# Routed expert blocks in pairs: TensorE's order of products, transposes and down products

## The reference

```python
scores = sigmoid(u @ w_router)                # 512 tokens, 64 experts
top_e  = ...                                  # 8 experts for each token, from the best 4 of 8 groups
wts    = scores[top_e] / sum * 2.5
# for each expert e and the tokens that chose it:
hid = silu(x @ we_gate[e]) * (x @ we_up[e])   # 1024 -> 256
y  += (hid @ we_down[e]) * wts                # 256 -> 1024
h   = h + g2 * (y + shared expert)
out = rmsnorm(h, final_norm_g)
```

## Time and profile before

| what | value |
|---|---|
| median of 3 executions | 2199.33 us (2198.82 to 2207.7) |
| the profiled execution | 2204.64 us, span 2202.8 us |
| mean granted TensorE clock | 0.990 |
| TensorE busy | 2139.4 us, 97% |
| VectorE, ScalarE, GpSimd busy | 55%, 33%, 38% |
| DMA | 358.78 MB, mean 163 GB/s |

### The profile page before, as it was taken

One profiled execution on the slowest core, in us unless ns is written; L12 is line 12 of the kernel. 1 busy time (PEld: TensorE's weight loads), 2 busy tenths in 40 slices (PEclk: granted clock), 3 DMA queues, 4 the chain that ended last, 5 costly groups with the idle time before them and its releaser, 6 DMA issues.

```text
span 2202.8 us, 31560 instructions
## 1 busy us (share of the span) xinstructions
PE 2139.4 (97%) x11812; PEld 1526.5 (69%) x11813; DVE 1214.1 (55%) x1894; ACT 716.2 (33%) x1116; POOL 839.5 (38%) x600
## 2 busy tenths in 40 slices
PE   6999999999989999999999999999999999999998
PEld 5877667787868777777777778876555555555554
DVE  6567665789991448599999684246421212121213
ACT  4335663333341324344444345223111111111112
POOL 4331023434443324334334356532144444444443
PEclk9999899999999999999999999999999999999999
DMA  5230122454544322333333313321768899999885
GB/s 166 77 96 1 68 77 77 148 196 153 191 144 144 105 60 78 105 101 102 104 101 101 96 58 114 116 101 77 293 221 289 302 335 307 319 341 343 318 296 195
DMA packets 172306, 358.78 MB, mean 163 GB/s; under 512 B 18785, under 2 KB 108001, under 8 KB 153393
## 3 DMA queue, kind: packets, MB, share of 16 engines
q1 hardware_dynamic: 136880, 256.81, 33.1%
q0 software_dynamic: 28336, 85.91, 12.6%
q10 hardware_dynamic: 6992, 14.75, 1.9%
HBM read 390.15 MB, written 33.10 MB: 192 GB/s over the span
## 4 chain that ended last, share of the span: by engine, by line
PE 85%; DMA 5%; DVE 3%; ACT 2%; POOL 2%; issue 1%; SPq 1%; ACTq 0%; POOLq 0%; DVEq 0%
PE bank L933 25%; PE bank L1667 14%; PE bank L1356 12%; PE bank L1688 7%; PE bank L1255 4%; PE bank L1435 3%; DMA arena<-in_we_gate 2%; PE bank L1646 2%; PE bank L1069 1%; PE bank L1442 1%; DMA arena<-in_w_up 1%; PE bank L1520 1%; PE bank L942 1%; PE bank L1104 1%; PE bank L950 1%
## 5 line engine op out<-in xcount | busy, mean ns | idle before, releaser
L1667 PE MATMUL bank<-arena,hn 128*64 128x256 f32 x3072 | 346.1, 384 | 6.2 <-DMA arena<-in_we_gate 5.5
L1667 PEld LDWEIGHTS bank<-arena,hn 128*64 128x64 f32 x3072 | 225.5, 139 | 139.0 <-issue 35.4
L813 POOL TENSOR_TENSOR w_low_flat<-arena,in_high 128x1024 fp32r<-128x1024 f32 x71 | 184.3, 2617 | 278.5 <-ACT in_high L1996 278.4
L2951 DVE TENSOR_TENSOR inv<-inv,bank 128x128 f32<-128x128 f32 x96 | 23.2, 283 | 321.4 <-PE bank L1667 321.4
L1688 PE MATMUL bank<-arena 128*64 128x512 f32 x768 | 175.4, 598 | 0.3 <-DVE arena L2957 0.3
L780 POOL TENSOR_TENSOR w_low<-arena,w_high 128x2048 fp32r<-128x2048 f32 x22 | 103.6, 4709 | 160.2 <-ACT w_high L1918 160.2
L1356 PE MATMUL bank<-in_x,in_high 128*128 128x512 f32 x384 | 154.2, 402 | 0.0
L2965 DVE SCALAR_TENSOR_TENSOR sq<-bank,arena 128x512 f32<-128x512 f32 x96 | 72.1, 751 | 148.6 <-PE bank L1688 143.7
L1356 PE MATMUL bank<-in_x,w_low_flat 128*128 128x512 f32 x384 | 151.1, 393 | 0.0
L1356 PE MATMUL bank<-x_low,in_high 128*128 128x512 f32 x384 | 150.7, 392 | 0.0
L933 PE MATMUL bank<-x_high,w_high 128*128 128x512 f32 x336 | 133.4, 397 | 1.9 <-POOL w_low L780 1.9
(11 more groups left out here) (506 smaller groups left out, 4912.5 us busy)
## 6 DMA issues: line engine op xcount, KB each, us to landing
arena<-in_we_gate SPq DMA_DIRECT2D x49, 1024.0 KB
arena<-in_we_up SPq DMA_DIRECT2D x49, 1024.0 KB
arena<-in_w_in SPq DMA_DIRECT2D x38, 1024.0 KB, 5.4
arena<-in_w_ada SPq DMA_DIRECT2D x12, 2048.0 KB, 8.0
arena<-in_w_up SPq DMA_DIRECT2D x22, 1024.0 KB, 10.7
arena<-in_w_in SPq DMA_DIRECT2D x17, 512.0 KB, 5.3
arena<-in_w_out SPq DMA_DIRECT2D x4, 2048.0 KB, 9.9
arena<-in_w_down SPq DMA_DIRECT2D x4, 2048.0 KB, 9.6
```

Source lines behind the costliest of these rows:

```text
L813: pool_eng.tensor_tensor(in2_tile(j, "low"), in2_tile(j, "whole"), in2_tile(j, "high").bitcast(f32), ALU.subtract).then_inc(S("w_low"), 1)
L1667: ins = nc.tensor.matmul(rows_of(banks[2 + part][:, 0:FE], c), columns_of(moe["xT"][:, p, :], k, c), moe["gu"][:, 2 * p + c, at:at + FE], ...
```

## The change

TensorE's order becomes: gate and up products of the pair's two blocks; then all transposes (the next pair's first block, half 0; hidden of the first block; half 1; the next pair's second block, half 0; hidden of the second block; half 1); then the down products of both blocks. The second block's down sums go to banks 3 and 1. The waits are set anew for the shared banks, and ScalarE's and VectorE's orders follow the pair. The orders of GpSimd and of the sync engine's queue are not in the diff. Its core:

```diff
+        DOWN_BANKS = ((5, 6), (3, 1))
...
@@ TensorE: block_transposes(b, p, gathers, half) @@
                 if half == 0:
                     pe.wait_ge(S(f"x_gathered{p}"), gathers * 16)
+                if p == 1:
+                    pe.wait_ge(S("xT_done"), b * 2 + (half - 1))
+                elif half == 1:
+                    pe.wait_ge(S("y_copied"), b * 2 + (2 * TT - 4))
@@ TensorE: block_up(b, p) @@
                     pe.wait_ge(S(f"{name}_in"), needed)
+                    if p == 0 and part == 1:
+                        pe.wait_ge(S("y_copied"), b * 2 + (2 * TT - 1))
+                    if p == 1:
+                        pe.wait_ge(*((S("gate_through"), b + 2) if part == 0 else (S("moe_hid"), b * 2)))
@@ TensorE: down_free is gone; the rest @@
-            def down_free(b, loaded, value):
-                pe.wait_ge(S(loaded), value)
-                for half in range(2):
-                    pe.wait_ge(S("y_copied"), b * 2 + (2 * TT + half - 1))
-
             def hidden_transposes(b, p):
+                if p == 1:
+                    pe.wait_ge(S("hT_done"), b * 2)
...
-            def block_down(b, p):
+            def block_down(b, p, loaded, value, copied=None):
+                pe.wait_ge(S(loaded), value)
                 for k in range(2):
                     pe.wait_ge(S("hT_done"), b * 2 + (k + 1))
                     for half in range(2):
+                        if k == 0 and half == 1 and copied is not None:
+                            pe.wait_ge(S("xT_done"), copied)
...
-                            ins = nc.tensor.matmul(rows_of(banks[5 + half], c), columns_of(moe["hidT"][:, p, :], k, c),
+                            ins = nc.tensor.matmul(rows_of(banks[DOWN_BANKS[p][half]], c), columns_of(moe["hidT"][:, p, :], k, c),
...
-            def block(b, p, gathers, loaded, value):
-
-                block_up(b, p)
-                block_transposes(b + 1, 1 - p, gathers, 0)
-                hidden_transposes(b, p)
-                down_free(b, loaded, value)
-                block_transposes(b + 1, 1 - p, gathers, 1)
-                block_down(b, p)
-
-            for half in range(2):
-                block_transposes(0, 0, 1, half)
-            block(0, 0, 1, "we_down_in", 32)
-            block(1, 1, 2, "we_down_in", 64)
+            def pair_rest(b, gathers, loaded, values):
+
+                block_transposes(b + 2, 0, gathers, 0)
+                hidden_transposes(b, 0)
+                block_transposes(b + 2, 0, gathers, 1)
+                block_transposes(b + 3, 1, gathers, 0)
+                hidden_transposes(b + 1, 1)
+                block_transposes(b + 3, 1, gathers, 1)
+                block_down(b, 0, loaded[0], values[0])
+                block_down(b + 1, 1, loaded[1], values[1], b * 2 + 8)
+
+            for p in range(2):
+                for half in range(2):
+                    block_transposes(p, p, 1, half)
+                block_up(p, p)
+            pair_rest(0, 2, ("we_down_in", "we_down_in"), (32, 64))
             with pe.Fori(1, pairs_but_one) as i:
 
-
-                for p in range(2):
-                    block(i * 2 + p, p, i + (p + 1), f"down_loaded{p}", i * 32)
-            block(pairs_but_one * 2, 0, pairs, "down_loaded0", pairs_but_one * 32)
-            block_up(pairs_but_one * 2 + 1, 1)
-            hidden_transposes(pairs_but_one * 2 + 1, 1)
-            down_free(pairs_but_one * 2 + 1, "down_loaded1", pairs_but_one * 32)
-            block_down(pairs_but_one * 2 + 1, 1)
+                block_up(i * 2, 0)
+                block_up(i * 2 + 1, 1)
+                pair_rest(i * 2, i + 2, ("down_loaded0", "down_loaded1"), (i * 32, i * 32))
+            for p in range(2):
+                block_up(pairs_but_one * 2 + p, p)
+                hidden_transposes(pairs_but_one * 2 + p, p)
+                block_down(pairs_but_one * 2 + p, p, f"down_loaded{p}", pairs_but_one * 32)
@@ ScalarE: the loop @@
-            with act.Fori(1, pairs) as i:
-                for b, p in ((i * 2 + (-1), 1), (i * 2, 0)):
-                    block_gate(b, p)
-                    block_rows(b + 1, 1 - p)
+            with act.Fori(1, pairs_but_one) as i:
+                for p in range(2):
+                    block_gate(i * 2 + p, p)
+                for p in range(2):
+                    block_rows(i * 2 + (2 + p), p)
@@ VectorE: block_out reads DOWN_BANKS[p][half]; the loop @@
-            with dve.Fori(1, pairs) as i:
-                for b, p, added in ((i * 2 + (-1), 1, i), (i * 2, 0, i + 1)):
-                    block_hidden(b, p)
-                    block_hidden_T(b, p)
-                    block_out(b, p, added)
+            with dve.Fori(0, pairs_but_one) as i:
+                for p in range(2):
+                    block_hidden(i * 2 + p, p)
+                for p in range(2):
+                    block_hidden_T(i * 2 + p, p)
+                for p in range(2):
+                    block_out(i * 2 + p, p, i + 1)
```

More of the change, by code:

```diff
@@ L2288, in _ @@
             pairs = pairs_but_one + 1
-            block_rows(0, 0)
-            block_gate(0, 0)
-            block_rows(1, 1)
-            with act.Fori(1, pairs) as i:
-                for b, p in ((i * 2 + (-1), 1), (i * 2, 0)):
-                    block_gate(b, p)
-                    block_rows(b + 1, 1 - p)
-            block_gate(pairs_but_one * 2 + 1, 1)
+            for p in range(2):
+                block_rows(p, p)
+                block_gate(p, p)
+            for p in range(2):
+                block_rows(2 + p, p)
+            with act.Fori(1, pairs_but_one) as i:
[4 more added lines that the diff above has]
+            for p in range(2):
+                block_gate(pairs_but_one * 2 + p, p)
             nc.scalar.activation(RECIP[:, 0:TT], EPS_COLUMN.to_broadcast([P, TT]), ACT.Sqrt)
@@ L2964, in block_out @@
                     dve.wait_ge(S(("moe_y", "down_through")[half]), b + (1 + 2 * half))
-                    nc.vector.scalar_tensor_tensor(moe["y"][:, p, 512 * half:512 * half + 512], banks[5 + half][:, :],
+                    nc.vector.scalar_tensor_tensor(moe["y"][:, p, 512 * half:512 * half + 512], banks[DOWN_BANKS[p][half]][:, :],
                                                    moe["wcol"][:, p:p + 1], moe["g2"][:, 512 * half:512 * half + 512],
@@ L2975, in _ @@
             pairs = pairs_but_one + 1
-            block_hidden(0, 0)
-            block_hidden_T(0, 0)
-            block_out(0, 0, 1)
-            with dve.Fori(1, pairs) as i:
-                for b, p, added in ((i * 2 + (-1), 1, i), (i * 2, 0, i + 1)):
-                    block_hidden(b, p)
-                    block_hidden_T(b, p)
-                    block_out(b, p, added)
+            with dve.Fori(0, pairs_but_one) as i:
+                for p in range(2):
+                    block_hidden(i * 2 + p, p)
+                for p in range(2):
+                    block_hidden_T(i * 2 + p, p)
+                for p in range(2):
+                    block_out(i * 2 + p, p, i + 1)
+            block_hidden(pairs_but_one * 2, 0)
+            block_hidden_T(pairs_but_one * 2, 0)
+            block_out(pairs_but_one * 2, 0, pairs)
             dve.wait_ge(S("w_known"), pairs_but_one * 2 + 3)
```

## The result

The changed kernel takes 2421.63 us (median of 4 executions, 2418.41 to 2430.11); the kernel before took 2201.83 us on the same chip. The ratio is 1.1002, with a 95% interval of [1.098, 1.1024]. It is slower, as forecast, but by 220 us where 140 were forecast, and 2421.63 lies 10 us above the stated range.

What follows compares the result with a forecast made beforehand. TensorE's order was the bound, with GpSimd's unchanged order now stalling it: 22 x (5.1 + 1.7) = +150 us, gaps -7, gate-weight waits -9, end +6, together +140, so about 2339 us; range 2252 to 2412.

Steps and rivals of the forecast that it cites:

- D to first scatter: GpSimd, from the end of the first block's down products (D) to that block's scatter starting: 4.9 us.
- interval of the scatters: GpSimd, start of a pair's first scatter to start of its second: 9.4 us, about halfway between 7.3 and 11.75.
- second scatter to gather: GpSimd, from the second scatter's start to the issue of the pair's second gather: 2.8 us.
- landing of the gather: Second gather, from issue to rows landed: 7.0 us taken; the chain's gather took 6.21, the upper estimate was 9.
- wanted at: When TensorE needs the second gather: 19.0 us after the end of the first block's down products.
- clock: TensorE after each stall runs mostly at 1.2 GHz instead of 2.4: 1.7 us more per pair.
- TensorE's gaps: Gaps before hidden transposes and down products go in the new order: 0.3 us gained per pair, 7 us in all.
- GpSimd's instructions alone: Rival: GpSimd's instructions alone set the stall, scatters land quietly, clock stays up; 22 x 3.5 us, 2266 us; chance 0.15.
- The waits for gate weights: TensorE's two waits for gate weights (5.5 us) and their slow stretches go: -9 us.
- The end: Tail of the kernel: the scatter of block 46 waits for that of block 45, +6 us.
- The signs: Expected in the trace: about 22 gather waits of 3 to 9 us, 28 to 33 us per pair, DMA share about 0.75.
- the contention does not thin out: Rival: scatter intervals of 11.75 us and a gather landing of 9; 22 x (9.4 + 1.7), 2433 us; chance 0.13.

Runs made afterwards that it cites:

- The first experiment: Changed kernel with GpSimd's loop alone reordered, both gathers for the next pair issued ahead of the down load and scatter: 2213.9 us, ratio 1.0062.
- shorter warm products: Changed kernel with 8 unread products of 512 columns put before TensorE's wait for the second gather: 2391.39 us, ratio 1.0871.
- light weights: Changed kernel with its loop's gate and up loads cut to one eighth of their bytes, GpSimd's order unchanged: 2307.32 us, ratio 1.0483.
- hidden transposes apart, first run: Kernel before, old order, with the second hidden transposes moved between the second and third block transposes of half 1: 2196.43 us, ratio 0.9987.

## Why the prediction was off

The direction and the mechanism were right: GpSimd's untouched order, with the second gather behind the first block's down products, makes TensorE wait in each of 22 pairs, and each wait costs clock as well. The first experiment shows it by moving two calls. The sum was too small by 80 us, and one term holds nearly all of it; the other misses cancel.

| term, per pair | predicted | measured |
|---|---|---|
| D to first scatter | 4.9 | 5.2 |
| interval of the scatters | 9.4 | 9.0 |
| second scatter to gather | 2.8 | 2.8 |
| landing of the gather | 7.0 | 10.5 |
| arrival | D+24.1 | D+27.5 |
| wanted at | D+19.0 | D+18.9 |
| clock | 1.7 | 2.3 |
| TensorE's gaps | -0.3 | -0.65 |
| period | 30.6 | 34.4 |

- **The step that failed is the landing of the gather**: "7.0 for the landing", chosen "because the longer pair thins the DMA traffic". It thins in the mean, 0.90 to 0.66 in the stage. But gate and up loads are set off by the products of the same pair, so they fall into D+7 to D+27, and the gather lands in a stretch at 0.87 in mean, 1.02 in the pair shown. The slack lies around the next D, before the next gathers are issued. With those loads cut to an eighth the same gather, at the same place, lands in 5.8 us. The 3.5 us between 7.0 and 10.5 make 77 of the 80 us. The share alone is not the whole of it. The row behind the 6.2 us is the stage's first gather: the DMA share was 0.92 in its flight, but nothing of GpSimd's stood ahead. In the loop a scatter does, and 8.1 of the 10.5 us pass until it has landed. My upper estimate of 9 had that wait and left out most of the 2.4 us behind it. How the 10.5 us divide between the loads and the queue was not tested apart. The trace of the kernel before held a nearer number: the 37 of its gathers in the loop for which most landing events are there take 8.7 us in mean.
- **The interval of the scatters** was right in sum (9.0), but for another reason: the first scatter is issued into the free stretch and takes 7.0 us, so it is mostly GpSimd's own 8.6 us that count, while the second takes 10.9. The rival "GpSimd's instructions alone" was right about this one term.
- **The clock** cost 2.3 us rather than 1.7. A pair with the gathers ahead needs 23.42 us of TensorE and the mean wait was 8.7 (27.6 less 18.9, with 0.4 for the first gather in it); 34.4 less both is 2.3. The slow stretch falls on transposes and down products here, on gate and up products in the earlier trace rows. The low clock came in each of the 22 turns (0.50 to 0.57 in the 4 us behind the wait). The Trainium skill, "TensorE: Matmul & The Clock Gate", "HAM oscillation — how this bites in real kernels", says so of its loop that waits for a DMA in each turn, and the trace agrees.
- **The gaps** were undersold: 0.65 us and not 0.3. The new waits for bank copies cost nothing that shows; in the gathers-ahead trace a pair's transposes take 2.58 us, below the 2.65 that I called the least.
- **The waits for gate weights** went, as said. **The end** cost 2.7 us, not 6.
- **The signs.** The 22 waits came, but of 4.2 to 12.9 us and not 3 to 9, and the share fell to 0.66 and not to 0.75. GpSimd was to wait for a landed scatter at most second scatters; it did so 6 times, 20.3 us in all.
- The rival "the contention does not thin out" (2433) came nearest in time by luck: the interval too long (11.75) and the landing too short (9) nearly made up for each other, as did its clock and its gaps. The Trainium skill's formula for such a DMA ("DMA: Bandwidth & Descriptors", "Anatomy of one DMA — SWDGE (gpsimd) path"), which gives 3.2 us for 512 KB, has no term for other traffic. It is near the gather at 1598.42 of the changed kernel, which took 3.4 us at a share of 0.25, though that one moved only some 0.23 MB. It is far from what a gather takes beside other traffic here; even with light weights it took 5.8.

## What to carry to other kernels

When one engine's order is changed, write down for every other engine's queue what it is waiting for at that moment; a queue that the diff leaves alone can turn a prefetch into a wait. Price a transfer with the DMA share of the stretch in which it will fly, not with the mean of the stage, and add what stands ahead of it in its own queue. And where two uses of a late resource move closer together, the second pays the difference, even if each buffer is as far from its last use as before.

## What the runs showed of the hardware

- TensorE's clock: an idle time of 1.30 us (shorter warm products) was followed by full clock; 2.64, 3.70 and 8.70 us were each followed by a slow stretch, and so was every one of the 22 waits for a second gather in the changed kernel. The idle time by itself does not decide: 2.10 us before 1729.71 (shorter warm products) was followed by 1.00, 2.09 us before 1780.25 (light weights) by 0.64, and 3.16 us before 1794.93 (hidden transposes apart, first run) by 1.00.
- A matmul of 512 columns with a 128 x 128 weight in 32-bit takes 0.43 us, one with 128 x 64 half of that: 16 of the first make 7.13 us, 32 of the second 7.09.
- The second gather of a pair, indirect, 128 rows (at most 512 KB), took 5.8 us in mean with the gate and up loads cut to an eighth and 10.5 us with them whole, both behind a scatter. With them whole it took 10.5 us right behind the first gather too. With nothing of GpSimd's ahead, the first gather of the stage took 5.8 us at a DMA share of 0.95.
- GpSimd's transfers (gathers, scatters, down loads) landed in the order of issue, all 141 of the changed kernel's routed stage, and likewise in the runs with other orders of GpSimd or with light weights.
